# The block inverse of a gated delta rule: two-row seeds and six doublings of 64-column products in place of eight-row seeds and four doublings of 128-column products

## The reference, cut to what matters

```python
a_low = jnp.where(strict, jnp.einsum('bnhie,bnhje->bnhij', kb, kc) * decay, 0.0)
lhs = a_low + jnp.eye(C, dtype=jnp.float32)
u = lax.linalg.triangular_solve(lhs, vb, left_side=True, lower=True)
w = lax.linalg.triangular_solve(lhs, kb * jnp.exp(gc)[..., None], left_side=True, lower=True)
```

## Time and profile before

| what | us |
|---|---|
| median of 3 runs | 2144.7 (2143.56 to 2146.27) |
| the profiled execution, its own time | 2143.65 |
| its span | 2141.7 |
| PE busy | 2074.2 (97%) |
| weight loads busy (beside PE) | 1143.4 (53%) |
| DVE busy | 978.9 (46%) |
| ACT busy | 327.8 (15%) |
| POOL busy | 50.3 (2%) |
| mean granted clock of PE | 0.996 |

### The profile page before, as it was taken

One profiled execution on the slowest core, in us unless ns is written; L12 is line 12 of the kernel. 1 busy time (PEld: TensorE's weight loads), 2 busy tenths in 40 slices (PEclk: granted clock), 3 DMA queues, 4 the chain that ended last, 5 costly groups with the idle time before them and its releaser, 6 DMA issues.

```text
span 2141.7 us, 24148 instructions
## 1 busy us (share of the span) xinstructions
PE 2074.2 (97%) x9716; PEld 1143.4 (53%) x9722; DVE 978.9 (46%) x1574; ACT 327.8 (15%) x729; POOL 50.3 (2%) x30
## 2 busy tenths in 40 slices
PE   6999999999999999999999999999999999999999
PEld 4858533333333333333333457868884658868874
DVE  1486444333333333333332256734676167626684
ACT  1142100000010000000000113302110113311110
POOL 0001000000000000000000002000000011000000
PEclk9999999999999999999999999999999999999999
DMA  9559389999999999999999834334442634334441
GB/s 371 218 195 365 113 359 417 427 428 428 428 428 426 428 428 427 429 426 429 427 428 427 307 133 158 139 105 157 146 145 97 224 121 158 110 126 155 148 157 51
DMA packets 133443, 593.52 MB, mean 277 GB/s; under 512 B 9774, under 2 KB 66270, under 8 KB 105178
## 3 DMA queue, kind: packets, MB, share of 16 engines
q1 hardware_dynamic: 133338, 592.02, 69.7%
HBM read 590.91 MB, written 3.18 MB: 277 GB/s over the span
## 4 chain that ended last, share of the span: by engine, by line
PE 81%; DMA 11%; DVE 5%; issue 1%; ACT 1%; POOL 1%; SPq 0%; POOLq 0%; DVEq 0%
PE bank L1624 24%; PE bank L679 22%; DMA ring<-in_w_dram 10%; PE bank L689 8%; PE bank L2751 6%; PE bank L2714 3%; PE bank L1765 2%; PE bank L1605 2%; PE bank L2729 2%; PE bank L962 2%; PE bank L3106 1%; PE bank L1641 1%; DMA ring<-in_w_ada_dram 1%; DVE arena L1289 1%; PE bank L593 1%
## 5 line engine op out<-in xcount | busy, mean ns | idle before, releaser
L1624 PE MATMUL bank<-ring,arena 128*64 128x512 f32 x2304 | 509.7, 594 | 11.4 <-DMA ring<-in_w_dram 9.9
L679 PE MATMUL bank<-wide,ring 128*128 128x256 f32 x2368 | 517.2, 381 | 2.8 <-ACT wide L2983 2.6
L679 PEld LDWEIGHTS bank<-wide,ring 128*128 128x128 f32 x2368 | 451.0, 191 | 67.5 <-issue 5.9
L1624 PEld LDWEIGHTS bank<-ring,arena 128*64 128x64 f32 x2304 | 161.1, 137 | 350.0 <-issue 322.4
L1265 DVE TENSOR_SCALAR arena<-bank 128x512 f32<-128x512 f32 x32 | 22.1, 692 | 376.3 <-PE bank L1624 376.3
L689 PE MATMUL bank<-ring,wide 128*128 128x512 f32 (+2 forms) x384 | 151.4, 554 | 0.0
L2411 DVE SCALAR_TENSOR_TENSOR arena<-bank,arena 128x254 f32<-128x254 f32 (+1 forms) x176 | 76.7, 477 | 84.3 <-ACT arena L2555 82.7
L689 PEld LDWEIGHTS bank<-ring,wide 128*128 128x128 f32 x384 | 72.6, 190 | 74.6 <-issue 71.3
L1269 DVE RECIPROCAL arena<-arena 128x512 f32<-128x512 f32 x32 | 107.3, 3353 | 1.1
L1441 ACT ACTIVATE arena<-arena 128x512 f32<-128x512 f32 x32 | 20.2, 631 | 492.9 <-DVE arena L1265 492.9
L1624 PE MATMUL bank<-wide,arena 128*64 128x512 f32 x392 | 89.0, 595 | 0.7 <-ACT arena L1445 0.7
(11 more groups left out here) (515 smaller groups left out, 1949.6 us busy)
## 6 DMA issues: line engine op xcount, KB each, us to landing
ring<-in_w_dram SPq DMA_DIRECT2D x144, 2048.0 KB, 24.1
wide<-in_w_dram SPq DMA_DIRECT2D x24, 2048.0 KB, 24.9
arena<-in_w_dram SPq DMA_DIRECT2D x22, 2048.0 KB, 27.0
ring<-in_w_up_dram SPq DMA_DIRECT2D x44, 1024.0 KB, 6.8
ring<-in_w_in_dram SPq DMA_DIRECT2D x21, 2048.0 KB, 8.1
ring<-in_w_ada_dram SPq DMA_DIRECT2D x12, 2048.0 KB, 9.0
ring<-in_w_down_dram SPq DMA_DIRECT2D x10, 2048.0 KB, 7.7
ring<-in_w_out_dram SPq DMA_DIRECT2D x6, 2048.0 KB, 8.4
```

What stands on the lines that cost most here:

```text
L679: ins = pe.matmul(B.bank(name, j)[:, i * T:(i + 1) * T], w[:, k, (first + i) * P:(first + i + 1) * P], hT[:, k, :], start=(k == 0), stop=( ...
L1624: ins = pe.matmul(bank[g * SLOTS:(g + 1) * SLOTS, :], lhsT, rhs[:, g * CH:(g + 1) * CH], start=start, stop=stop)
```

## The change

The inverse now starts from 2 x 2 diagonal blocks, which need no product (I - A), and has six doublings, of blocks of 2 to 64. In a doubling only every other block of columns changes, so each product reads and writes 64 of 128 columns. In front of each four, PE multiplies a constant by a constant: 256 columns of bfloat16 into the unused half of the bank. The third part of `mod` is cut into 8 pieces that stand between the products of the first four doublings. The projection `z` and its `silu` are split: token tile 0 at the old place, tile 1 after the transposes of A (PE) and after the doublings (DVE). ACT, not DVE, scales V and K while copying. POOL makes the identities and clears the five `T1` buffers. On SP, one load of `w_ada` goes last, the broadcast of the third part of `mod` waits for `u1`, and `layer_params` goes behind the wait for `dno`.

```diff
+LEVELS = 6
...
-                    ("o0", 1), ("t1", 4), ("o1", 1), ("tv", 2), ("kk", 2), ("kq", 2), ("aT", 2), ("ag2", 1),
-                    ("p2", 4), ("p4", 2), ("zz", 4), ("xx", 4)):
+                    ("o0", 1), ("t1", 4), ("o1", 1), ("tv", 2), ("kk", 2), ("kq", 2), ("aT", 2), ("z1", 1), ("ag2", 1)):
...
+        def ada_row(pe, g, piece):
...
+            for i in range(4):
...
+                    ins = pe.matmul(rows[32 * i:32 * i + 32, :], silu_c[:, 2 * a + k, :], split(w, 2)[:, k, i * CH:(i + 1) * CH],
+                                    start=False, stop=(piece == (1, 1)))
...
+            if g == 2:
+                sp.wait_ge(*B.ready("u1"))
...
         def delta_pool(pool):
...
+            pool.memset(t1_at[0], 0.0).then_inc(S["t1z"], 1)
...
+            pool.tensor_tensor(Xm, everywhere(ident, 8), everywhere(ident, 8), ALU.mult).then_inc(S["unit"], 1)
...
+                if lv > 1:
+                    pool.wait_ge(*B.ready(f"bx{lv - 2}", 1))
+                pool.tensor_tensor(BT[lv % 2], AT, everywhere(c(f"low{lv}"), 8), ALU.mult).then_inc(S["bmat"], 1)
...
+        def z_silu_v(v, then, tt):
...
+            then(v.tensor_scalar(e, e, 1.0, None, ALU.add))
+            then(v.reciprocal(e, e))
+            ins = v.tensor_tensor(dz[:, tt, :], dz[:, tt, :], e, ALU.mult)
...
         def delta_v(v, then):
...
+                v.scalar_tensor_tensor(out=d, in0=s_, scalar=-1.0, in1=where_, op0=ALU.mult, op1=ALU.mult)\
+                 .then_inc(S["e_mat"], 1)
+                v.wait_ge(S["e_mat"], 2 * odd + 1)
+                v.tensor_tensor(d, d, one, ALU.add).then_inc(S["e_mat"], 1)
...
+            for lv in range(LEVELS):
+                for n, j in enumerate(XJOBS if lv < LEVELS - 1 else XJOBS[1::2]):
...
+                    v.tensor_tensor(m, m, narrow(half4(f"xl{lv}", n), lv), ALU.subtract).then_inc(B.free(f"xl{lv}", n), 1)
+
+            z_silu_v(v, then, 1)
...
         def delta_s(act):
...
+            act.wait_ge(S["vb"], 3)
+            zrow_s(act, 1)
+            for lv in range(LEVELS):
+                act.wait_ge(S["t1z"], (1, 2, 2, 3, 4, 5)[lv])
+                for j in range(2):
+                    act.wait_ge(*B.ready(f"bx{lv}", j))
+                    act.activation(tile_level(T1[lv], j, lv, 0), narrow(half4(f"bx{lv}", j), lv), ACT.Copy)\
+                       .then_inc(B.free(f"bx{lv}", j), 1)
             act.wait_ge(S["mod_out"], 16)
             ada_rows_s(act, 2)
...
         def delta_t(pe):
...
-            ada_rows_t(pe, 2)
-            pe.wait_ge(S["e_mat"], 2)
...
+            zrow_t(pe, 1)
+            pe.wait_ge(S["e_mat"], 4)
+
+            def half(name, i, one, tt):
+
+                pe.wait_ge(*B.room(name, i))
+                pe.matmul(B.bank(name, i)[:, 2 * P:CH], plain[:, 0:P], plain[:, 0:2 * P], start=True, stop=True)
+                for hd in range(4):
+                    ins = one(half4(name, i)[:, hd, :], 4 * tt + hd)
+                ins.then_inc(B.full(name, i), 1)
...
+            ada_row(pe, 2, None)
+            third = [(a, k) for a in (0, 2, 3, 1) for k in range(2)]
+            for lv in range(LEVELS):
...
+                for tt in range(2):
+                    if lv:
+                        pe.wait_ge(*B.taken(f"xl{lv - 1}", 2 * tt))
+                    half(f"bx{lv}", tt, half_product(BT[lv % 2], Xm, lv, 0), tt)
+                if lv < 4:
+                    ada_row(pe, 2, third[2 * lv])
+                for tt in range(2):
+                    pe.wait_ge(*B.taken(f"bx{lv}", tt))
+                    if lv:
+                        pe.wait_ge(*B.taken(f"xl{lv - 1}", 2 * tt + 1))
+                    if not last:
+                        half(f"xl{lv}", 2 * tt, half_product(XTm, t1, lv, 0), tt)
+                    half(f"xl{lv}", tt if last else 2 * tt + 1, half_product(t1, XTm, lv, 1), tt)
+                    if tt == 0 and lv < 4:
+                        ins = ada_row(pe, 2, third[2 * lv + 1])
...
+            for n in [n for n in range(N1) if n != last_in] + [last_in]:
...
                 if ch == 4:
 
+                    sp.wait_ge(S["dno"], 1)
                     layer_params(sp, 0, late=False)
-                    sp.wait_ge(S["dno"], 1)
...
             result_v(v, then, B, S, jobs1[0], 0, att[:, 0, :], den[0], flag="attn_p")
+            v.wait_ge(S["gexp"], 1)
+            v.tensor_tensor(bg, beta, egc, ALU.mult).then_inc(S["vb"], 1)
+            z_silu_v(v, then, 0)
             result_v(v, then, B, S, jobs1[1], 1, att[:, 1, :], den[1], flag="attn_p")
...
             turned_qk_t(pe)
-            rows_of("z", n + 2)
+            zrow_t(pe, 0)
             ada_rows_t(pe, 1)
```

More of the change, by code:

```diff
@@ L76, in add, with add_beside @@
         for _ in range(count):
+            b = self.n % 8
+            self.n += 1
+            self.bank.append(b)
+            self.nth.append(self.used[b])
+            self.used[b] += 1
+    def add_beside(self, name, count, kept):
+        self.at[name] = len(self.bank)
+        for _ in range(count):
+            if self.n % 8 == kept:
+                self.n += 1
             b = self.n % 8
@@ L137, in constants @@
     parts["early"] = -BIG * (f < p)
[L138 to L141, removed]
+    masks = {}
+    for lv in range(-1, LEVELS):
+        L = 2 << lv if lv >= 0 else 1
+        masks[f"low{lv}"] = (p // (2 * L) == f // (2 * L)) & ((f // L) % 2 == 1) & ((p // L) % 2 == 0)
+    for lv in range(3, LEVELS):
+        parts[f"low{lv}"] = masks[f"low{lv}"]
     for qt in range(TT):
@@ L169, in constants @@
     parts["bucket"] = (np.arange(P)[:, None] == bucket[None, :])
+    parts["pair"], parts["pairT"] = masks["low-1"], masks["low-1"].T
+    for lv in range(3):
+        parts[f"low{lv}"] = masks[f"low{lv}"]
     where, at, cols = {}, 0, []
@@ L333, in c @@
             at, n = CW[name]
+            if at >= NCON:
+                return area(15360 + at - NCON, n)[0:rows, :]
             return con[0:rows, at:at + n]
@@ L713, in everywhere @@
         def everywhere(mask, n):
-            return mask.unsqueeze(1).to_broadcast([P, n, P])
+            return mask.unsqueeze(1).to_broadcast([P, n, mask.shape[1]])
         def tile4(m, tt):
@@ L720, in b4, with half4, level @@
             return split(B.bank(name, i)[:], 4)
+        def half4(name, i):
+            return split(B.bank(name, i)[:, 0:2 * P], 4)
         XJOBS = (0, 2, 1, 3)
-        def delta_pool(pool):
[L727 to L734, removed]
+        def level(m, lv, odd):
+            if lv < 0:
+                return m.rearrange("p (b two) -> p b two", two=2)[:, :, odd]
+            L = 2 << lv
+            return m.rearrange("p (b two r) -> p b two r", two=2, r=L)[:, :, odd, :]
@@ L794, in delta_v, with pairs @@
                 ins.then_inc(B.free("kk", tt), 1)
+            def pairs(dst, src, mask, odd):
+                one, where_ = everywhere(level(ident, -1, odd), 8), everywhere(level(c(mask), -1, odd), 8)
+                d, s_ = level8(dst, odd), level8(src, odd)
+                v.scalar_tensor_tensor(out=d, in0=s_, scalar=-1.0, in1=where_, op0=ALU.mult, op1=ALU.mult)\
+                 .then_inc(S["e_mat"], 1)
+                v.wait_ge(S["e_mat"], 2 * odd + 1)
+                v.tensor_tensor(d, d, one, ALU.add).then_inc(S["e_mat"], 1)
+            for tt in range(TT):
+                v.wait_ge(*B.taken("kk", tt))
+            v.wait_ge(S["unit"], 1)
+            pairs(Xm, Am, "pairT", 0)
             for tt in range(TT):
@@ L805, in delta_v @@
[L805 to L843, removed]
+            v.wait_ge(S["unit"], 2)
@@ L976, in delta_t @@
                 four("aT", tt, lambda out, u: pe.transpose(out, Am[:, u, :], ident), tt)
-            ada_rows_t(pe, 2)
-            pe.wait_ge(S["e_mat"], 2)
[L979 to L994, removed]
-                    four(name, n, (product(XTm, rhs), product(rhs, XTm))[j // 2], j % 2)
@@ L997, in delta_t @@
-            updates("zz", XJOBS, P2, None)
-            updates("xx", XJOBS, P4, "zz")
-            for lv in range(4):
-                last = f"xl{lv - 1}" if lv else "xx"
-                pe.wait_ge(S["bmat"], lv + 1)
-                for j in range(2):
-                    for i in range(2):
-                        pe.wait_ge(*B.taken(last, 2 * j + i))
-                    four(f"bx{lv}", j, product(BT, Am), j)
-                jobs = XJOBS if lv < 3 else XJOBS[1::2]
-                for n, j in enumerate(jobs):
-                    if n % (len(jobs) // 2) == 0:
-                        pe.wait_ge(*B.taken(f"bx{lv}", j % 2))
-                    four(f"xl{lv}", n, (product(XTm, T1), product(T1, XTm))[j // 2], j % 2)
+            zrow_t(pe, 1)
@@ new lines, in delta_t @@
+            pe.wait_ge(*B.room("ag2"))
+            ada_row(pe, 2, None)
+            third = [(a, k) for a in (0, 2, 3, 1) for k in range(2)]
+            for lv in range(LEVELS):
+                t1, last = T1[lv], lv == LEVELS - 1
+                pe.wait_ge(S["bmat"], lv + 1)
```

(14 more changed lines are left out.)

141 lines of the change are left out of this document (104 added, 37 removed), and 1 row of the table p.

## The result

The changed kernel takes 2152.31 us (median of 9 runs, of which eight lie between 2151.17 and 2153.63 and one, of 7766.82 us, plays no part in the ratio), the kernel before 2146.27 us beside it (9 runs). The ratio is 1.0030 [1.0022, 1.0039]: 6 us slower, where I forecast no change (2144.6, range to 2151.5). So about 4 of the 10 us that the two traces differ by are scatter of single executions.

A forecast was written before the change was run, and what follows sets the result against it. PE was taken to bound the kernel, busy 2074.2 of 2141.7 us. The parts, 1.6 - 2.2 + 0.5 = -0.1 us, on the profiled 2143.65 us, plus 1.05 to the median, gave 2144.6 us, range 2138.5 to 2151.5.

The forecast's parts named there:

- part 1: Ahead of the inverse: moving z for tile 1 delays the inverse's start by 1.6 us, bounds +0 and +3.5.
- the gap at 139 us: In PE's stream, where z for tile 1 leaves 6.87 us: later work moves forward by 5.2 us, not all of it.
- rival C: Clock falls in the new inverse or the stage after, where PE streams less: +6 us, 2150.6 us; chance 0.14.
- Part 2: The inverse, from the bias of mod to its last wait: 41.6 us against 43.8, so -2.2 us.
- Part 3: SP's queue: biases land later behind `layer_params`, and PE's second turn of x waits: +0.5 us, bounds 0 and +4.
- Rival D: SP's queue: biases come later than 251.5 us and DVE delays PE's turns: +4, 2148.6 us; chance 0.12.
- Rival B: Inverse: columns count, a 64-column record costs half of 0.112 us; about 2132.5 us; chance 0.06.
- Rival E: Constant products cost full column time and more (+3), gap at 139 us not closed (+1.7): 2149.3 us; chance 0.10.

The follow-up runs named there:

- Experiment 1: The changed kernel with 15 constant bfloat16 products of 512 columns put ahead of three PE waits in front of the inverse: 2147.84 us, 1.0007.
- Experiment 2: The changed kernel with POOL's identity for X made later, not beside DVE's scaling of K: 2147.35 us, 1.0004.
- experiment 3: The changed kernel with POOL's identity for X made later and 8 constant products in PE's waits ahead of the attention of tile 1: 2146.58 us, 1.0003.
- experiment 4: The changed kernel with z for both tiles and the third mod part whole at their old places, SP's loads in natural order: 2142.09 us, 0.9983.
- experiment 5: The kernel of experiment 4 with the three bias loads ahead of `layer_params` on SP: 2143.41 us, 0.9988.
- experiment 8: The kernel of experiment 7 with every product of the inverse streaming 128 columns instead of 64: 2140.67 us, 0.9975.
- experiment 7: The kernel of experiment 5 without the 34 constant products of 256 columns: 2140.95 us, 0.9976.

## Why the prediction was wrong

**The step that failed** is part 1, the move of z, put at +1.6 us with a ceiling of +3.5; it cost 8.4 in the trace. I asked whether the gap at 139 us closes, found that it closes all but 1.6 us, and took the rest of the front at its old durations. Three things were not followed:

- The waits that remain. PE waits 1.74, 0.70 and 1.52 us between 152 and 161.5 us, since the z that had kept it behind DVE and ACT was gone. I used the 1.00 of the earlier trace rows over L628 as evidence against rival C, although that row stands behind 13.73 us of 512-column products, half of which the change takes away. The clock fell, and that cost 4.7 us. Rival C had the mechanism and the price (+6; 2150.6 us) and a chance of 0.14, but I looked for it in the inverse, and even named 175 to 250 us as the place where it would show. It came at 161 to 171. Experiment 1 shows it.
- POOL. I looked at when its clears and identities would be ready, not at whom they would stand beside. The identity at 151.19 us held DVE for 1.7 us on the path. Experiment 2 shows it. Without the two, the front would have cost 8.4 - 4.7 - 1.7 = 2.0 us, and in experiment 3, which is without the two, it cost 1.4. So the 1.6 for the gap itself was sound; what the forecast had at nothing were the clock and POOL.
- The same overlap comes back with POOL's masks of level 0 beside DVE's seeds (2.38 and 2.72 us instead of 0.69). z for tile 1 covers it, by less than 0.4 us (181.82 against 182.18).

**Part 2** had the right sign and half the size, -1.0 for -2.2. After: 0.99 (bias) + 8 x 0.995 (pieces) + 34 x 0.84 (fours) + 4.7 (constants: 25 at 0.11, 9 that stand behind a mod piece at 0.22) + 0.63 (last wait) = 42.8 us. Predicted: 1.0 + 7.0 + 30.3 + 2.7 + 0.6. A four with its constant takes 0.95 us, as I had (0.97). The missing term is the break: a mod piece among the fours costs 0.99 us and not 0.875, and the constant behind it twice as much, together 8 x 0.12 + 9 x 0.11 = 1.95 us, of which experiment 4, without pieces, gives 1.8 back. The pieces were meant to fill waits, and no waits were there: in experiment 4 DVE and ACT keep up without them. No wait for masks or cleared buffers came in.

**Part 3** held in its sum, but by luck: two errors in it cancel. Timeline of SP's queue after, and the chain where the biases are read, answering to the earlier trace rows:

```profile
227.51 2.02 SPq L2980 DMA_DIRECT2D ring<-in_w_dram  x4
243.66 0.71 SPq L2181 DMA_DIRECT2D arena<-in_conv_w_dram  x2
...
249.16 0.90 SPq L2977 DMA_DIRECT2D arena<-in_b_dram  x2
```

```profile
250.10 6.74 DMA arena<-in_b_dram
256.86 1.22 DVE arena L1211
...
258.57 0.70 DVE wide L1219
```

All is about 9 us later, since `u0` is. The biases were issued 24.2 us behind `u0`; I had 28.9 (244.5 - 215.6), since I took 10 us for the ten small loads ahead of them, which were issued in 5.5 (243.66 to 249.16). From the first issue they took 7.7 us to land (249.16 to 256.86), not 3.7. So DVE reads them 31.9 us behind `u0`, and I had 32.4. The cost to the first expert was 0.3 us for a predicted 0.5. Rival D is out; experiment 5 puts SP's order at about 0.5 us.

**Rival B** (columns count) is out by experiment 8. The Trainium skill (TensorE: Matmul & The Clock Gate, Back-to-back issue gap) lists a smaller gap for 64 columns than for 128 for a product by itself, and says that in a stream of weight loads and products both set the spacing. For these f32 products, whose weights change each time, the two widths measured alike, 0.112 us, as the second of these would have it. **Rival E** had its halves: the constants were cheap (0.055, I took 0.08), the gap at 139 us closed about as forecast.

**The best version** that the runs gave is experiment 7 or 8: 2140.95 and 2140.67 us, 5 us below the kernel before and 11 below the change. Against experiment 4 (2142.09) their intervals overlap.

## What to carry to other kernels

Dense work that is moved out of a stretch with waits takes the clock's cover with it: before moving it, list PE's waits in the stretch that it leaves, with the work gone, and price a fall there (here 4.7 us), not only at the place where the work goes. When work is newly given to POOL, ask which DVE instruction with two SBUF inputs runs at that time. And put pieces between short products only where the trace shows a wait to fill, for each break in the stream has a price of its own.

## What the runs showed of the hardware

- Two engines on one port pair: DVE's 1.22 us became 2.92 beside a POOL product of two SBUF inputs, while the scaling just before it (`L864`) stayed at 1.23 beside POOL's clear (`L792`, at 150.28 us), and DVE's decay rows, which read one of their tensors from PSUM, showed 0.34 us each beside POOL's 1.90 us product of experiment 2, the same as with POOL idle.
- f32 products with new 128 x 128 weights come every 0.112 us at 64 and at 128 columns. With a bfloat16 product of 256 columns after every eight, a four and its constant take 0.953 instead of 0.898 us: half of the constant's 0.11 us in the chain hides beside the next weights.
- The granted clock at the start scatters between the traced executions of these kernels, with nothing changed in that part of the program (0.50, 0.67, 0.70, 0.83, 1.00 in the same 10 us), and the 8-column products begin up to 4.6 us apart. A single trace of each kernel can't settle 6 us; the length of each stage, from its own start, can.
